# First mixer's projections in three split passes with row-by-row blended inputs, and the modulation sums of two layers moved beside other stages

## The reference

```python
def first_block(...):
    mod = silu(c) @ w_ada + b_ada                    # six vectors of 1024: "layer 0"
    ...                                              # attention, SSD branch, w_out: the mixing
    x = layer_norm(ALPHA * x + gate1 * mixed)
    x = layer_norm(ALPHA * x + gate2 * peer_ffn(x * (1 + scale2) + shift2))
def second_block(x, ...):
    for i in range(2):
        mod = silu(c) @ ada_w[i] + ada_b[i]          # "layer 1" and "layer 2"
        h = rms(x) * (1 + sc1) + sh1
        y = rwkv7_mix(h) if i == 0 else mlstm_mix(h)
        x = x + g1 * y
        x = x + g2 * swiglu(rms(x) * (1 + sc2) + sh2)
    return rms(x) * final_w
def rwkv7_mix(x, mix, w_in, ...):
    xx = token_shift(x) - x
    xs = x + xx * mix[n]                             # six blended inputs, n = 0..5
    r, k, v = xs[0] @ w_r, xs[2] @ w_k, xs[3] @ w_v  # 1024 x 1024 each
    wl, al, gl = xs[1] @ w_w, xs[4] @ w_a, xs[5] @ w_g  # 64, 64 and 160 columns
    ...
```

## Time and profile before

| what | us |
| --- | --- |
| median of 3 runs (lowest, highest) | 4645.68 (4644.84, 4654.81) |
| the profiled execution's own time | 4643.22 |
| its span | 4641.5 |
| PE busy in the span | 4171.2 |
| DVE busy | 2388.3 |
| ACT busy | 1560.5 |
| POOL busy | 1450.9 |

### The profile page before, as it was taken

One profiled execution on the slowest core, in us unless ns is written; L12 is line 12 of the kernel. 1 busy time (PEld: TensorE's weight loads), 2 busy tenths in 40 slices (PEclk: granted clock), 3 DMA queues, 4 the chain that ended last, 5 costly groups with the idle time before them and its releaser, 6 DMA issues. The chain is left out here.

```text
span 4641.5 us, 66658 instructions
## 1 busy us (share of the span) xinstructions
PE 4171.2 (90%) x25838; PEld 3310.6 (71%) x25838; DVE 2388.3 (51%) x4600; ACT 1560.5 (34%) x2088; POOL 1450.9 (31%) x601
## 2 busy tenths in 40 slices
PE   5999996869999999999999959799978988997988
PEld 3777774748888888788888824388857865776866
DVE  6776765867886888433333365456533213433211
ACT  2445443213334444322222210144324412433421
POOL 2323322324443333344444400011124431323432
PEclk9999997989999999999999979899989999998999
DMA  3222326833334555555555516300013321211321
GB/s 149 100 96 85 106 75 233 298 102 129 129 127 154 181 181 181 178 192 184 188 186 191 166 58 192 96 3 3 3 37 95 95 105 48 66 54 64 99 98 55
DMA packets 272559, 555.17 MB, mean 120 GB/s; under 512 B 16712, under 2 KB 150472, under 8 KB 267376
## 3 DMA queue, kind: packets, MB, share of 16 engines
q1 hardware_dynamic: 272368, 552.55, 35.5%
HBM read 472.71 MB, written 79.77 MB: 119 GB/s over the span
## 5 line engine op out<-in xcount | busy, mean ns | idle before, releaser
L1678 POOL TENSOR_TENSOR peer_wl<-peer_wf,peer_wh 128x1024 fp32r<-128x1024 f32 x272 | 706.3, 2597 | 986.8 <-ACT peer_wh L1691 986.8
L1765 PE MATMUL peer_y<-peer_xh,peer_wh 128*128 128x512 f32 x1152 | 455.9, 396 | 29.8 <-DVE peer_xl L1837 29.8
L1691 ACT ACTIVATE peer_wh<-peer_wf 128x1024 fp32r<-128x1024 f32 x272 | 286.4, 1053 | 547.5 <-PE peer_y L1767 518.3
L1767 PE MATMUL peer_y<-peer_xh,peer_wl 128*128 128x512 f32 x1152 | 449.4, 390 | 0.0
L1766 PE MATMUL peer_y<-peer_xl,peer_wh 128*128 128x512 f32 x1152 | 449.4, 390 | 0.0
L1796 PE MATMUL peer_y<-peer_twh,peer_wh 128*128 128x512 f32 x1024 | 405.3, 396 | 11.0 <-DVE peer_twl L1905 11.0
L1797 PE MATMUL peer_y<-peer_twl,peer_wh 128*128 128x512 f32 x1024 | 405.1, 396 | 0.0
L1798 PE MATMUL peer_y<-peer_twh,peer_wl 128*128 128x512 f32 x1024 | 404.9, 395 | 0.0
L659 POOL TENSOR_TENSOR br_wl<-br_wf,br_wh 128x1024 fp32r<-128x1024 f32 x80 | 197.2, 2465 | 420.7 <-ACT br_wh L861 420.7
L1962 POOL TENSOR_TENSOR up_wl<-up_wf,up_wh 128x1024 fp32r<-128x1024 f32 x88 | 211.2, 2400 | 342.6 <-ACT up_wh L1991 342.6
L1977 PE MATMUL up_acc<-up_xh,up_wh 128*128 128x512 f32 x704 | 275.8, 392 | 47.0 <-DVE up_xl L2027 47.0
(11 more groups left out here) (516 smaller groups left out, 8961.1 us busy)
## 6 DMA issues: line engine op xcount, KB each, us to landing
peer_wf<-in_u SPq DMA_DIRECT2D x128, 512.0 KB, 3.3
peer_wf<-in_v SPq DMA_DIRECT2D x128, 512.0 KB, 3.5
up_wf<-in_w_gu SPq DMA_DIRECT2D x88, 512.0 KB, 3.5
br_wf<-in_w_in SPq DMA_DIRECT2D x80, 512.0 KB, 3.2
mix_aw<-in_w_ada SPq DMA_DIRECT2D x40, 1024.0 KB, 7.2
acts<-peer_aout SPq DMA_DIRECT2D x128, 256.0 KB, 2.0
gates<-peer_gout SPq DMA_DIRECT2D x16, 2048.0 KB, 7.3
peer_gout<-gates SPq DMA_DIRECT2D x32, 1024.0 KB, 7.7
```

The lines of the kernel that those rows point to most:

```text
L1678: nc.gpsimd.tensor_tensor(wl[:, t % SLOTS], wf[:, t % 2], wh[:, t % SLOTS], ALU.subtract).then_inc(w_low, 1)
L1691: nc.scalar.activation(wh[:, t % SLOTS], wf[:, t % 2], ACT.Copy).then_inc(w_high, 1)
L1765: nc.tensor.matmul(out, wh[:, slot, k], xh[:, k], start=(k == 0), stop=False)
L1767: last = nc.tensor.matmul(out, wl[:, slot, k], xh[:, k], start=False, stop=(k == KT - 1))
```

## The change

- `mix_phase` keeps only the 16 halves of layer 0, spread over tiles 1 to 20.
- Layer 1's sums go to the expert values: 24 pieces of 1 MB (512 columns, 4 row tiles; `ada_piece`) into `C.H`, 96 single steps on DVE (`ada_step`), one for each of tiles 8 to 103; the 48 column matmuls and the bias (`add_bias`) at the phase's end.
- Layer 2's sums go to the first up phase: the same 24 pieces, spread over slots 2 to 19 (`pieces`): slots 2, 3, 4 get pieces [0], [1], [2, 3], slots 5, 6, 7 get [4], [5], [6, 7], and so on. DVE makes them after the slot's `hid_l`, SP loads two ahead, PE makes the columns at the head of the next slot, once the odd piece is done. The up phases' loops on SP, PE and DVE are written out.
- `rwkv_project_phase` is new: small projections first (plain float32), then 24 weight tiles in three passes; the blended rows are made one at a time in 4 stage buffers, rounded on ACT into rings of 12 rows, with the rest on DVE.

```diff
+PIECES = 24
+def ada_piece(io, layer, n):
+    c, h = divmod(n, 2)
+    return io["w_ada"][12 * layer + c][:, 4 * h:4 * h + 4]
+def ada_step(nc, acc, out, w, csil, k):
+    if k == 0:
+        return nc.vector.tensor_scalar(acc, w, csil[:, 0:1], None, ALU.mult)
+    return nc.vector.scalar_tensor_tensor(out=out if k == KT - 1 else acc, in0=w, scalar=csil[:, k:k + 1], in1=acc,
+                                          op0=ALU.mult, op1=ALU.add)
+def add_bias(nc, C, link, layer, sums):
+    at = 48 * layer
+    link(nc.vector.tensor_tensor(C.mod[:, at:at + 48], sums, C.v("b_ada", at, 48), ALU.add))
+    for part_n in (1, 4):
+        col = at + 8 * part_n
+        link(nc.vector.tensor_scalar(C.mod[:, col:col + 8], C.mod[:, col:col + 8], 1.0, None, ALU.add))
-MIX_ADA = 40
+MIX_ADA = 16
-    LAST_ADA = 28
+    LAST_ADA = 20
...
# peer_phase, SP, at the end of value tile e's turn
+                    if e % 4 == 1 and (e - 5) // 4 in range(PIECES):
+                        n = (e - 5) // 4
+                        if n >= 2:
+                            sp.wait_ge(stepped, 4 * (n - 1))
+                        sp.dma_start(C.H[:, 4 * (n % 2):4 * (n % 2) + 4], ada_piece(io, 1, n)
+                                     ).then_inc(piece_loaded[n % 2], 16)
# PE, after the last value tile
+                pe.wait_ge(stepped, 12 * KT)
+                pe.wait_ge(x_done, 1)
+                for c in range(12):
+                    for n in range(4):
+                        last = nc.tensor.matmul(banks[:, 0, 4 * c + n:4 * c + n + 1], part_of(c)[:, n * P:(n + 1) * P],
+                                                C.ones[:, 0:1], start=True, stop=True)
# DVE, after the rest of value tile e
+                    if step_at(e) is not None:
+                        c, k = divmod(step_at(e), KT)
+                        n = 2 * c + k // 4
+                        if k % 4 == 0:
+                            dve.wait_ge(piece_loaded[n % 2], 16 * (n // 2 + 1))
+                        ...
+                        ada_step(nc, part_of(c), part_of(c), C.H[:, 4 * (n % 2) + k % 4], C.csil[:, 8:16], k
+                                 ).then_inc(stepped, 1)
...
# up phase, SP; load_piece(n) waits for stepped >= 4 * (n - 1)
-                    with sp.Fori(0, ROUNDS) as i:
+                    for i in range(ROUNDS):
                         for b in range(BANKS):
+                            if b % 2 == 0:
+                                at = 2 * i + b // 2
+                                if layer == 0 and at == 1:
+                                    load_piece(0)
+                                    load_piece(1)
+                                for n in pieces(at - 2):
+                                    if n + 2 < PIECES:
+                                        load_piece(n + 2)
# PE
+                    def columns(c):
+                        pe.wait_ge(stepped, KT * (c + 1))
+                        ...                             # four matmuls of one column
+                    for i in range(ROUNDS):
                         for b in range(BANKS):
+                            if b % 2 == 0:
+                                for n in pieces(2 * i + b // 2 - 1):
+                                    if n % 2:
+                                        columns(n // 2)
# DVE, after hid_l of slot 2 * i + n
+                            for m in pieces(2 * i + n):
+                                steps(m)
...
# rwkv_project_phase, PE
+                for n, width in enumerate((64, 64, P)):
+                    for k in range(KT):
+                        pe.wait_ge(small_mixed, KT * n + k + 1)
+                        last = nc.tensor.matmul(sacc[0:width, n], ws[:, k, at:at + width], small[n][:, k],
+                                                start=(k == 0), stop=(k == KT - 1))
+                ...
+                product(nc, sacc[0:32, 3], ws[:, :, 256:288], small[2], KT).then_inc(small_done, 1)
+                for t in range(TILES):
+                    n, slot = t // KT, t % SLOTS
+                    pe.wait_ge(w_low, t + 1)
+                    if t >= BANKS:
+                        pe.wait_ge(kept, t - BANKS + 1)
+                    for k in range(KT):
+                        j = KT * n + k
+                        if t % KT == 0:
+                            pe.wait_ge(x_low, j + 1)
+                        nc.tensor.matmul(out, wh[:, slot, k], xh[:, j % RING], start=(k == 0), stop=False)
+                        nc.tensor.matmul(out, wh[:, slot, k], xl[:, j % RING], start=False, stop=False)
+                        last = nc.tensor.matmul(out, wt[:, slot, k], xh[:, j % RING], start=False, stop=(k == KT - 1))
+                        if t % KT == KT - 1 and k < KT - 1:
+                            last.then_inc(freed, 1)
# DVE
+                for j in range(len(BIG_MIXES) * KT):
+                    n, k = divmod(j, KT)
+                    mix(stage[:, j % STAGE], BIG_MIXES[n], k).then_inc(mixed, 1)
+                    if j:
+                        low(j - 1)
```

More of the change, by code:

```diff
@@ L1946, in swiglu_phases, with pieces @@
             ROUNDS = FF_TILES // 2
+            def pieces(at):
+                n = PIECES * (at - 2) // 18
+                end = PIECES * (at - 1) // 18
+                return range(n, end) if layer == 0 and 2 <= at < 20 else range(0)
             with ph.block() as block:
@@ L2027, in _, with steps @@
                         nc.vector.tensor_tensor(xl[:, k], C.H[:, k], xh[:, k], ALU.subtract).then_inc(x_low, 1)
-                    with dve.Fori(0, ROUNDS) as i:
+                    link = Chain(dve, chain_s)
+                    def steps(n):
+                        c, h = divmod(n, 2)
+                        dve.wait_ge(piece_loaded[h], 16 * (c + 1))
+                        if h == 0 and c >= 2:
+                            dve.wait_ge(columns_s, c - 1)
+                        for k in range(4 * h, 4 * h + 4):
+                            if k:
+                                dve.wait_ge(stepped, KT * c + k)
+                            ada_step(nc, asum[:, c % 2], part[:, c % 2], C.H[:, k], C.csil[:, 8:16], k
+                                     ).then_inc(stepped, 1)
+                    for i in range(ROUNDS):
                         for n in range(2):
@@ L2045, in rwkv_project_phase @@
 def rwkv_project_phase(nc, io, C, rkv, wl, al, gl, gl2):
+    TILES, SLOTS, BANKS, STAGE, RING = 24, 2, 4, 4, 12
+    DECAY_MIX, A_MIX, G_MIX = 1, 4, 5
+    BIG_MIXES = (0, 2, 3)
     with Phase(nc, "rwproj") as ph:
[L2048 to L2051, removed]
@@ L2052, in rwkv_project_phase @@
-        ws = ph.sb("ws", [P, KT, 288])
[L2053 to L2061, removed]
+        loaded = [ph.sem(f"loaded{r}") for r in range(SLOTS)]
@@ L2159, in _, with high @@
+                def high(j):
+                    act.wait_ge(mixed, j + 1)
+                    if j >= RING:
+                        n, k = divmod(j - RING, KT)
+                        act.wait_ge(freed, (KT - 1) * n + k + 1) if k < KT - 1 else act.wait_ge(projected, KT * (n + 1))
+                    nc.scalar.activation(xh[:, j % RING], stage[:, j % STAGE], ACT.Copy).then_inc(x_high, 1)
+                w_highs(0)
+                w_highs(1)
                 act.wait_ge(small_done, 1)
                 nc.scalar.activation(wl[:], sacc[0:64, 0], ACT.Tanh)
+                for j in range(KT):
+                    high(j)
@@ L2165, in _ @@
                 nc.scalar.activation(gl2[:], sacc[0:32, 3], ACT.Sigmoid)
+                for t in range(TILES):
+                    n, m = divmod(t, KT)
+                    if m == KT - 1 and n < 2:
+                        for k in range(RING - KT, KT):
+                            high(KT * (n + 1) + k)
+                    w_highs(t + SLOTS)
+                    if t + SLOTS >= TILES:
+                        act.wait_ge(projected, t + 1)
+                    nc.scalar.activation(rkv[:, t], acc[:, t % BANKS], ACT.Copy).then_inc(kept, 1)
+                    if m == 1 and n < 2:
+                        for k in range(RING - KT):
+                            high(KT * (n + 1) + k)
 RW_PAIRS = KT
```

187 lines of the change are left out of this document (93 added, 94 removed).

## The result

The changed kernel takes 4719.72 us (median of 4 runs, 4717.94 to 4720.29); the kernel before takes 4650.25 beside it. The ratio is 1.0146, 95% interval 1.0131 to 1.0161. Slower was right; 4670 was 50 us short, and the range ended at 4705. The profiled execution took 4719.7, span 4718.0, which is 76.5 above the span of before. The sum is made against spans, as the forecast's was.

What follows compares the result with a forecast made beforehand. No engine was taken to bound the whole kernel; each stage had its own limit. Minus 66 (mixing), minus 71.8 (projections), plus 2.7 (expert values) and plus 159.2 (first up phase) gave plus 24: 4670 us, range 4618 to 4705.

Steps and rivals of the forecast that it cites:

- The sign and the mechanism: Whole kernel slower, chance 0.70: in the first up phase PE waits 12 times for DVE's sums, and weight tiles come late.
- Mixing: Mixing phase: fewer sums and loads let it end near 919, 65.5 us sooner; bounds minus 52 to minus 82.
- the projections: First mixer's projections: three passes and no sums, 167.2 us instead of 239, minus 71.8; bounds minus 62 to minus 75.
- the expert values' loop: Expert values: the added DVE steps and loads are covered, 0 us; without the cover at most 75 us of DVE.
- part 4: First up phase, the deciding term: plus 159 us from PE's waits, lost clock and late tiles; bounds 104 to 185.
- The 3.7 a wait: First up phase: slow columns and half-pace matmuls after each of 12 waits, 12 x 3.7 = 44.4 us.
- the 48 columns of the expert values: End of the expert values: columns take 12.3 us, with the bias plus 2.7; at half clock plus 13.
- PE's waits cost no clock: Rival, first up phase: the waits bring no slow matmuls, minus 34 on its term, 4636 us; chance 0.07.
- PE's waits are short: Rival, first up phase: sums done before PE reaches the next slot, about 4525; partly right 4600 to 4636; chance 0.10.
- The up phase loses more: Rival, first up phase: late tiles as in the upper bound of 185, 4696 us or more; chance 0.2.
- The projections gain little: Rival, projections: hand-overs pace each row, 24 rows at 1.5 exposed, 36 us, 4705 us; chance 0.05.
- Mixing gains more: Rival, mixing phase: PE's pace throughout, minus 16 more, 4654 us; with other small errors chance 0.13.

Runs made afterwards that it cites:

- experiment 3: Changed kernel with PE's columns one slot later and the piece loads behind the weight tiles in the first up phase: 4542.77 us, ratio 0.9765.
- experiment 2: Changed kernel with only the piece loads moved behind the weight tiles in the first up phase: 4680.85 us, ratio 1.0065.
- Experiments 6 and 7: Changed kernel, one edit each: POOL's up-phase weight split in four instructions, 4694.9 us; DVE's sum steps ahead of `hid_l`, 4664.02 us.
- Experiment 8: Changed kernel without 24 of the 48 column matmuls at the end of the expert values: 4708.26 us, ratio 1.0119.
- experiment 5: Changed kernel with 40 to 56 wide matmuls into a spare bank ahead of each of the 12 column waits: 4704.13 us, ratio 1.011.
- experiment 9: Changed kernel with the projections of the kernel before (plain float32, old order), without sums in them: 4758.25 us, ratio 1.0226.

## Why the prediction was short

**The sign and the mechanism were right.** PE's in-order queue behind DVE's sums, SP's loads ahead of the weight tile, ACT and silu behind that tile, slow matmuls after each wait: all are in the trace, the waits and slow matmuls 12 times and the delay by a late tile six times, and experiment 3 takes them away and 177 us with them. Mixing was 1.4 off, the projections 2.1, the expert values' loop 1.1. In the mixing, the split of tile 9 was forecast done near 786 and was done at 785.4:

```profile
783.02 2.34 POOL L1312 TENSOR_TENSOR mix_wl<-mix_wf,mix_wh 128x1024 fp32r<-128x1024 f32 x1 [7.76 <-ACT mix_wh L1350]
```

**The step that failed** is the reading of one row in part 4: "`hid_l` at 3726.68, done 3727.37". The row itself says 2.36 us, and 0.69 was the duration of the same operation where nothing runs beside it. With 2.36 read as it stands, a wait is 5.55 + 1.67 = 7.2 and 8.65 + 1.67 = 10.3; experiment 2 measures 7.14 and 10.38. Nor was the row an exception: over both up phases of the kernel before, the operation had a median of 2.30 (ns: least, median, most).

```profile
L2036 DVE TENSOR_TENSOR hid_l<-up_prod,hid_h x44: 692/2302/2356, 3509.1 to 4469.7; 128x512 f32 x44
```

Of the up phase's 33 missing us:

- The six waits with two pieces: 62.2 instead of 51.9, plus 10.3, `hid_l` alone.
- The six with one piece: 70.7 instead of 33.3 + 21.6 = 54.9, plus 15.8. The longer `hid_l` of the slot before makes the tile later by 1.6 each time. Three times ACT loads a table twice, 2.56 instead of the 1.3 that I took, and `hid_l` itself is long. Experiments 6 and 7 move just these terms.
- The start: 6.4 instead of 4.9.
- Clock and columns, and all else in the phase: 192 less the 139.4 of the 13 waits is 52.6, where 44.4 + 2.5 + 0.7 was forecast, plus 5. The 3.7 a wait were nearly right (columns 1.87, 8 to 14 slow matmuls).

So this step makes up 22 of the 50 us by which the forecast was short (10.3 and 15.8, less 3 x 1.28 for the second table load). With the row read as it stands in all 12 waits, 12 x 1.67 = 20 more, the forecast would have been 4690: the step was the largest miss, not the only one.

**Second, the 48 columns of the expert values.** I took 24 in 6.28, 0.26 each, and named 0.47 each as the bound, plus 13. They took 0.38 to 0.44; the clock fell under them, and the norm behind them began slow (its first 16 matmuls took 9.58, before 8.63): plus 11.7 in all, 9 over the forecast. Experiment 8 shows that the columns set that end, by 7.9 us. The rest, 5.7 in the heads and behind the up phase, was not followed up; experiment 3's execution was 6 us off behind the up phase too.

**The rivals.** "PE's waits cost no clock" is out: the mean clock is 0.80 and experiment 5 gets 16 back. "PE's waits are short" was out for this kernel, and its 4525 is close to what experiment 3 reaches by another order of the queues, 4543. "The up phase loses more" is what happened, and worse than its 185, since that bound kept the short `hid_l`. "The projections gain little" is out: it would have cost 36 us, and 2.1 were missing. "Mixing gains more" is out too: minus 64.1, not the 16 more. My split of their gain was never stated in the prediction; experiment 9's expectation gave the passes 33 to 40 us, and they have 37.7.

## What to carry to other kernels

Put work that consumes a slow side product one slot behind the work that makes it, on every in-order queue: PE's columns and SP's loads one slot later turned plus 70 us into minus 107, with the same instructions. And take the duration of an instruction from the row at the very place where it will stand on the path; the same operation elsewhere may have had no neighbour. Where two engines' instructions end together, ask which one holds the other.

## What the runs showed that I had not expected

**A VectorE operation held by GpSimd.** `hid_l` (two inputs in SBUF, 128x512) takes 0.69 us alone. Where it begins some 0.5 us after a GpSimd subtraction of 2.4, it takes 2.34 to 2.48, and each time it ends 0.54 to 0.56 after POOL's instruction. Where it begins 0.38 before the end of one, it takes 0.93. Beside the same subtraction in pieces of 0.735 it takes 0.69 to 0.82. If the two shared the way to SBUF as long as they overlap, the pieces would not have helped. GpSimd is held as well: a piece that begins while `hid_l` runs takes 1.17 to 1.20. DVE's `up_prod`, with one of its inputs in PSUM, took 0.69 at 3434.06 while POOL ran, and the sum steps, whose sum lies in PSUM, took 0.78 each beside it; neither was held. The Trainium skill, GPSIMD Engine Reference, Specifications, says that GpSimd's SBUF interfaces are shared with VectorE and that instructions with two SBUF inputs contend; the trace agrees.

**The clock under narrow matmuls.** It fell to 1.2 GHz at the end of the expert values with PE busy on one-column matmuls and an idle time of only 1.10 us ahead of them. In experiment 5 it fell after idle times of only 0.9 us with 4 columns, in some cases and not in others of the same kernel, and not after some of 2.3 and 2.5. In experiment 3 the same 4 columns without idle time cost no clock, 12 times. Why the one and not the other stays open. The Trainium skill, TensorE: Matmul & The Clock Gate, HAM oscillation, speaks of idle gaps; here the clock fell with hardly any.
